# Sixty-four tokens of the second expert layer on fetched rows, the other 192 with merged high and low parts

## The reference

```python
q = (t @ w_q).reshape(b * n, PEER_HEADS, 2, PEER_KEY_DIM)        # 8 heads, keys of 128
s = jnp.einsum('thcd,hcnd->thcn', q, sub_keys)
sv, si = lax.top_k(s, PEER_TOPK)                                 # 16 of 128, twice
cand = (sv[:, :, 0, :, None] + sv[:, :, 1, None, :]).reshape(b * n, PEER_HEADS, PEER_TOPK * PEER_TOPK)
score, pos = lax.top_k(cand, PEER_TOPK)
expert = i1 * PEER_KEYS + i2                                     # of 16384 experts
gate = jax.nn.softmax(score)
act = gelu(einsum('td,thkd->thk', tb, take(u_tab, eb, axis=0)))
out = einsum('thk,thkd->td', gb * act, take(v_tab, eb, axis=0))
```

## Time and profile before

| | us |
|---|---|
| median of 3 runs | 3408.69 (3408.18 to 3410.98) |
| the profiled execution, its own time | 3414.44 |
| its span, first to last instruction | 3412.5 |
| PE busy | 3245.4 |
| DVE busy | 2377.2 |
| ACT busy | 1434.5 |
| POOL busy | 1061.1 |

### The profile page before, as it was taken

One profiled execution on the slowest core, in us unless ns is written; L12 is line 12 of the kernel. 1 busy time (PEld: TensorE's weight loads), 2 busy tenths in 40 slices (PEclk: granted clock), 3 DMA queues, 4 the chain that ended last, 5 costly groups with the idle time before them and its releaser, 6 DMA issues.

```text
span 3412.5 us, 53827 instructions
## 1 busy us (share of the span) xinstructions
PE 3245.4 (95%) x20582; PEld 2965.5 (87%) x20582; DVE 2377.2 (70%) x3931; ACT 1434.5 (42%) x1708; POOL 1061.1 (31%) x670
## 2 busy tenths in 40 slices
PE   7999889998999999999989999999988999999998
PEld 5999689755877999999989999997778999988787
DVE  6877477786753689988649989986664965016665
ACT  5435344323533333466523333324344468444443
POOL 0110000010000477777654335540001976740000
PEclk9999899999999999999999999999999999999999
DMA  8874157451022377799999999983114669768875
GB/s 318 334 295 167 50 203 247 160 191 50 1 75 93 116 270 244 260 374 382 361 349 390 381 391 409 409 337 111 38 61 156 230 210 307 257 233 288 305 287 205
DMA packets 305190, 814.27 MB, mean 239 GB/s; under 512 B 21760, under 2 KB 188928, under 8 KB 253696
## 3 DMA queue, kind: packets, MB, share of 16 engines
q1 hardware_dynamic: 241856, 583.07, 47.4%
q0 software_dynamic: 58752, 213.94, 16.6%
q10 hardware_dynamic: 4416, 15.05, 1.1%
HBM read 722.84 MB, written 89.13 MB: 238 GB/s over the span
## 4 chain that ended last, share of the span: by engine, by line
PE 76%; DVE 14%; DMA 5%; ACT 2%; issue 2%; POOL 0%; SPq 0%; DVEq 0%; ACTq 0%; POOLq 0%
PE ps L2747 18%; PE ps L3060 11%; PE ps L3052 9%; PE ps L861 7%; PE ps L1687 5%; PE ps L872 4%; DMA arena<-activations 3%; PE ps L2309 3%; PE ps L318 3%; PE ps L1429 2%; PE ps L2769 2%; PE ps L1411 2%; DVE arena L2785 2%; PE ps L2149 1%; PE ps L977 1%
## 5 line engine op out<-in xcount | busy, mean ns | idle before, releaser
L2747 PE MATMUL ps<-xT_split,arena_split 128*128 128x384 f32 (+1 forms) x4096 | 917.1, 312 | 17.1 <-POOL arena_split L2720 10.4
L2720 POOL TENSOR_TENSOR arena_split<-ring,arena_split 128x1024 fp32r<-128x1024 f32 x256 | 631.7, 2477 | 932.7 <-ACT arena_split L2674 931.6
L2747 PEld LDWEIGHTS ps<-xT_split,arena_split 128*128 128x128 f32 x4096 | 698.1, 191 | 18.6 <-issue 15.8
L2747 PE MATMUL ps<-hT_split,arena_split 128*128 128x384 f32 (+1 forms) x2048 | 635.4, 310 | 0.0
L3060 PE MATMUL ps<-arena_split 128*128 128x384 f32 x3072 | 535.4, 335 | 11.6 <-DVE arena_split L3012 11.6
L3060 PEld LDWEIGHTS ps<-arena_split 128*128 128x128 f32 x3072 | 534.8, 188 | 12.2 <-issue 11.7
L285 DVE TENSOR_TENSOR arena_split<-ring,arena_split 128x2048 fp32r<-128x2048 f32 x128 | 292.9, 2291 | 247.4 <-ACT arena_split L279 246.6
L2985 ACT ACTIVATE arena_split<-ring 128x2048 fp32r<-128x2048 f32 x128 | 245.5, 1918 | 492.3 <-PE ps L3060 283.3
L279 ACT ACTIVATE arena_split<-ring 128x2048 fp32r<-128x2048 f32 x128 | 244.5, 1915 | 379.1 <-PE ps L861 133.3
L2747 PEld LDWEIGHTS ps<-hT_split,arena_split 128*128 128x128 f32 x2048 | 392.3, 192 | 0.0
L3009 DVE TENSOR_TENSOR arena_split<-ring,arena_split 128x2048 fp32r<-128x2048 f32 x128 | 293.1, 2290 | 99.5 <-ACT arena_split L2985 98.5
(11 more groups left out here) (318 smaller groups left out, 5098.5 us busy)
## 6 DMA issues: line engine op xcount, KB each, us to landing
ring<-in_weights SPq DMA_DIRECT2D x396, 1024.0 KB
arena<-in_side_weights POOLq DMA_DIRECT2D x152, 512.0 KB, 5.6
gates<-arena SPq DMA_DIRECT2D x48, 512.0 KB
arena<-gates SPq DMA_DIRECT2D x32, 768.0 KB
arena<-activations SPq DMA_DIRECT2D x64, 384.0 KB
activations<-arena SPq DMA_DIRECT2D x128, 128.0 KB
gates<-arena SPq DMA_DIRECT2D x16, 1024.0 KB
arena<-gates SPq DMA_DIRECT2D x64, 256.0 KB
```

Source lines behind the costliest of these rows:

```text
L2720: pool.tensor_tensor(low, self.raw(f)[:, j, :], high.bitcast(F32), ALU.subtract)\
L2747: mm = pe.matmul(k.ps[:, j, 0:self.T], self.u[:, 2 * (f % 2) + j, a, t * P:(t + 1) * P], self.h[b][:, t, :], start=n == 0, stop=n == 3 * D ...
```

## The change

Layer two now takes the fetched way for its first 64 tokens and the dense way for the other 192 (`SPREAD = 64`, `T = 192`). Each of the 64 tokens is spread over two partitions, 64 picked rows on each, so that there are 64 fetches of u and 64 of v, each 128 rows of 4 KB (512 KB). `dots_of` takes the dot products in the lot stretch, at lot `n` all rows `s` with `24 * s // 64 <= n` (two or three a lot). Seven row buffers in the hidden stage, five in the values stage.

For the 192 dense tokens the high and low parts of the activations lie side by side, and one product with the high weights streams both (384 columns); a second product takes the low weights with the high activations (192 columns). So a half is 16 products, not 24. The high-times-low part lands in PSUM beside the rest and must be added: ACT copies it out (L2808) and PE adds it back with a product with the identity (`fix`, in the middle of the next half) before the gelu. In the values stage v is now the weight in the same two products, and a 64-column product with a 0/1 `selector` adds the fetched rows' sum; `PeerAddSpread` adds each of eight tiles to x as soon as PE has it.

The gates are built in 24 lots, one a pair in pairs 28 to 51 (`ROUTE_PAIRS` 24 becomes 28), and 12 pairs follow without lots. In these stretches DVE takes low parts off POOL: those of every second pair in the lot stretch, and all after it (`on_dve`). The copy of x to DRAM and back is dropped in layer two. In layer one nothing moves but that the lot stretch is written out, not looped.

```diff
-ROUTE_PAIRS = (32, 24)
+ROUTE_PAIRS = (32, 28)
+LOTS_PER_PAIR = (2, 1)
...
+class SpreadHidden:
+    N_BUFFERS = 7
...
+        self.lot_of = [lots * s // self.n for s in range(self.n)]
...
+    def gpsimd(self, pool, pair):
+        hidden, rows = self.hidden, self.k.io["u_rows"]
+        first = hidden.route_pairs // 2
+        if pair < first:
+            return
...
+        while self.issued < self.n:
+            s, b = self.issued, self.issued % self.N_BUFFERS
+            before = s - self.N_BUFFERS
+            ready = first + s if before < 0 else hidden.route_pairs + self.lot_of[before] // hidden.per_pair + 2
+            if ready > pair and pair < hidden.pairs - 1:
+                return
+            if before >= 0:
+                pool.wait_ge(self.dotted.sem, self.dotted.at(before + 1))
+            pool.indirect_dma_start(self.buffers[b], None, rows, bass.IndirectOffsetOnAxis(self.index[:, s:s + 1], 0),
+                                    element_offset=P * P * D).then_inc(self.landed[b].sem, 16)
+            self.issued += 1
...
+    def dots_of(self, dve, lot):
+        while self.taken < self.n and self.lot_of[self.taken] <= lot:
+            s = self.taken
...
+            dve.wait_ge(landed.sem, landed.at(16 * (s // self.N_BUFFERS + 1)))
+            dve.scalar_tensor_tensor(row, row, 1.0, self.own, ALU.mult, ALU.mult, accum_out=self.dots[:, s:s + 1])\
+               .then_inc(self.dotted.sem, 1)
...
+    def on_dve(self, c):
+        if not self.merged:
+            return False
+        return c >= self.lots_to or c >= self.route_pairs and (c - self.route_pairs) % 2 == 1
...
             for j in range(2):
                 pool.wait_ge(self.u_high.sem, c * 2 + self.u_high.at(j + 1))
+                if c and self.on_dve(c - 1):
+                    pool.wait_ge(k.chunk_products, c + self.g)
...
+        for c in range(self.pairs):
+            if not self.on_dve(c):
                 body(c, c, 0, 4)
+            self.gather.gpsimd(pool, c)
...
+        def merged_products(c, f, j):
...
+            for t in range(DT):
+                pe.matmul(both, self.u[:, u, 0, t * P:(t + 1) * P], self.h_both[:, t], start=t == 0, stop=True,
+                          skip_group_check=True)
+                mm = pe.matmul(both[:, 1, :], self.u[:, u, 1, t * P:(t + 1) * P], self.h_both[:, t, 1, :], start=False,
+                               stop=True, skip_group_check=True)
+                if t == 3 and (j or not first(c, 1)):
+                    fix(c * 2 + (j - 1), 1 - j)
...
+            if self.merged:
+                gather.dots_of(dve, n)
+                c = self.route_pairs + n
+                if self.on_dve(c):
+                    u_lows(c)
...
+        def u_lows(c):
+            for j in range(2):
+                dve.wait_ge(self.u_high.sem, self.u_high.at(2 * c + j + 1))
+                dve.wait_ge(k.chunk_products, c + self.g)
```

More of the change, by code:

```diff
@@ L2607, in walk @@
     def walk(self, eng, body, between=None, lots=None, after=None):
-        def both(*pair):
-            for j in range(2):
-                body(*pair, halves=(j,))
-                lots(*pair, halves=(j,))
         if body:
@@ L2743, in body @@
                     pe.wait_ge(self.gelus.sem, c * 2 + self.gelus.at(j - 1))
+                if self.merged:
+                    merged_products(c, f, j).then_inc(self.u_products.sem, 1)
+                    if isinstance(c, int) and c == self.pairs - 1 and j:
+                        fix(c * 2 + 1, 1)
+                    continue
                 n = 0
@@ L3022, in vector @@
             self.gather.add(dve, PAIRS)
+            self.finish(dve, (self.back, 16), (self.products, self.pairs))
         else:
-            walk(dve, 0, self.pairs, 4, body)
-        self.finish(dve, (self.back, 16), (self.products, self.pairs))
+            self.gather.select(dve)
+            n = self.gather.rows_total
+            for c in range(self.pairs):
+                body(c, c, 0, 4)
+                self.gather.add(dve, n * c // (self.pairs - 4) if c < self.pairs - 4 else n)
+            self.finish(dve)
     def gpsimd(self, pool):
```

412 lines of the change are left out of this document (276 added, 136 removed).

## The result

The change makes the kernel slower: 3493.03 us median of four runs (3483.68 to 3511.63) beside 3409.84 (3408.18 to 3415.75), ratio 1.0242, 95% interval 1.0207 to 1.0276. The profiled execution took 3489.81 us, its span 3488.0, where the prediction's sum for the profiled execution was 3425.4. So 64 us are to be found.

The account below looks back on a forecast made before the run. PE was taken to end last in all three stretches, POOL close behind while routing. Hidden +37, gap +3, values -28, end -1 give +11 us on 3408.7: 3419 us, slower by 0.3%, range 3375 to 3455.

Parts of the forecast that it names:

- The sign: Whole kernel: slower, by 0.3%; slower by more than 0.2% had a chance of 0.47.
- the ring: Lot stretch: DVE low part, POOL low parts, row fetch, dots and lots wait in a circle, 18.5 to 20 us each turn.
- L: Lot stretch: time from POOL issuing an even lot's last row until DVE takes it, set at 5.0 us.
- The price of 192 columns: PE, hidden and values stages: a product 192 columns wide takes 0.112 us, between 0.093 and 0.120.
- the time from the last ring to the end of the hidden products: Hidden stage: from 3012, pair 51 done at 3019, then twelve pairs without lots in 57 us, ending at 3077.
- the gap ahead of the values stage: Between hidden and values stages: 8.3 us before, plus 1.2 for the last fix and 1.7 for fetches beside gate loads.
- the end: After the values stage: turn and copies go, adds per tile outrun PE's last pair; 9.5 us instead of 10.5.
- Step one: Values stage: transfers of 2.0 MB set the pace at 4.95 us a pair, above PE, two buffers and DVE; 325.5 us.
- Step two: Lot stretch: an odd lot's two or three rows have landed when DVE needs them, so its dots take 2.5 or 3.75 us.
- The rival with late rows: Lot stretch: rows land as late as with loaded queues; L = 8 makes 3452 us, 12.9 makes 3506; chance 0.15.
- Step three: End of routing: DVE's routing has a few small instructions more, done by 2752; POOL sets the pace, first lot at 2783.
- T: Lot stretch: moment DVE has made the first low part of an odd pair; 2797 at pair 29, 3012 at pair 51.

Follow-up runs that it names:

- 4: Changed kernel with each u row from the eighth on issued one pair earlier in the hidden stage: 3440.24 us, ratio 1.0069.
- 5: Changed kernel with POOL making all low parts in the lot stretch and DVE none: 3439.97 us, ratio 1.0086.
- 1: Changed kernel with layer two's values-stage activations loaded ahead of the next 1 MB chunk, not behind it: 3455.04 us, ratio 1.012.
- 2: Changed kernel without 59 of the 64 fetches of v rows, DVE adding the first five again and again: 3458.14 us, ratio 1.0123.
- 3: Changed kernel with values-stage activations loaded ahead of the chunk and 59 of 64 v row fetches left out: 3456.91 us, ratio 1.0127.
- 7: Changed kernel with POOL waiting, ahead of each routing low part, for its own last one, leaving a gap: 3490.65 us, ratio 1.0231.
- 10: Changed kernel with activations loaded first, u rows a pair earlier, POOL waiting for DVE at two places and gaps in eight pairs: 3389.8 us, ratio 0.9926.

## Why the prediction was wrong

**What was right.** The sign, to which the prediction gave no more than 0.47, and the mechanism with the highest weight: the ring stands in the trace with all its links, L is 5.0 in the mean, as taken, PE is busy 64% in it (about 60% forecast), and two cuts at different links (4, 5) both open it. The price of 192 columns (0.1116), merged and low product together 0.286 us from start to start, the time from the last ring to the end of the hidden products (68 us for 65), the gap ahead of the values stage (9 for 11), the end (7.3 for 9.5).

**Step one that failed: the values stage, "Transfers ... That is the largest"**, 35 us. The list of what could set a pair's pace had PE, two buffers, DVE and bytes; it left out how long a transfer takes from issue to landing when its issue itself waits for the work two pairs back. Shown by 1: the order of two loads alone moves the stage from 360 to 321. The trace of before held the circle too, hidden. SP's last small load of a turn, the use that waits for it, and DVE's next low part:

```profile
3203.63 0.33 SPq L2957 DMA_DIRECT2D arena<-gates  x1
...
3208.72 0.69 DVE L3007 TENSOR_TENSOR arena<-arena 128x512 f32<-128x512 f32 x1 [0.41 <-DMA arena<-gates]
...
3210.86 2.29 DVE L3009 TENSOR_TENSOR arena_split<-ring,arena_split 128x2048 fp32r<-128x2048 f32 x1 [1.44 <-ACT arena_split L2985]
```

A turn took 10.88 us there (3202.18 to 3213.06, twice PE's 5.44 a pair), of which DVE stood 1.44 for ACT: the circle alone was some 9.4, 4.7 a pair. It came up for two reasons: PE's share fell to 4.6, and with the fetches of rows in the queues the time from issue to landing grew from 5.1 us (3203.63 to 3208.72) to 6.6 to 8.7. Take either away, the order (1) or the rows' bytes (2), and the stage falls to 321. The 4.95 us a pair is near the 5.0 of experiment 1 only by chance: without the rows' bytes and with the loads first the two buffers still give 4.83 (3), so most of it is not bytes.

**Step two: "whose rows were issued 1.2, 2.4 and 3.6 us later and have landed meanwhile"**, 20 us. They had not. The rows that an odd lot waited for, second to fourth of a burst, were used 7.4 to 10.7 us after their issue, where the ring as drawn leaves the fourth some 7.6 (by its own terms), and DVE stood 1.7 us a ring for them; POOL waits 0.45 more for ACT's second high part. So a ring takes 21.3, not 19.5. The rival with late rows had the direction but the wrong place: the first row of a burst landed as forecast, the ones issued behind it late.

**Step three: the start of the lots**, 11 us at pair 29 (T at 2808.4, not 2797). "DVE's routing has a few small instructions more" counted DVE's work and not what POOL does to it. Before, POOL stood 0.15 to 0.57 us for ACT ahead of 23 of its 50 low parts up to 2769. The instruction that is held took 2.36 and 2.26 us in its two executions of layer two, both times until the low part in progress ended and such a gap came (the expectation of 7 gives 0.29 and 2.36; the 0.29 is not of layer two):

```profile
2664.62 2.40 POOL L2720 TENSOR_TENSOR arena_split<-ring,arena_split 128x1024 fp32r<-128x1024 f32 x1 [0.47 <-ACT arena_split L2674]
2664.82 2.36 DVE L2809 TENSOR_TENSOR arena<-arena 128x128 f32<-128x128 f32 x1
2667.51 2.46 POOL L2720 TENSOR_TENSOR arena_split<-ring,arena_split 128x1024 fp32r<-128x1024 f32 x1 [0.48 <-ACT arena_split L2674]
```

The change made PE faster than POOL, so these gaps closed. That gaps prevent the long hold is shown: 7 and 10 change only when POOL's low parts start, and in the profiles of the six kernels with such gaps all 12 executions in layer two took 0.3 to 2.3 us, while 9 of the 16 in the eight kernels without them took 29 to 34. Why the other 7 of those got their turn within 1.2 us, also beside a stream without gaps, stays open. The rest of the late start, some 6 us (lots begin 162.2 us after POOL's first low part in 10, 156.1 in the forecast), is still there with few gaps; ACT's exponentials stand behind high parts of pair 28 in its order and DVE needs 6 us from them to the first lot, but no run took this apart.

The ring cost (21.3 - 15.6) x 11 = 63 us in the trace and 53 in the time (in the profile of 4 two instructions were held, and its lots began 9.5 us later), the circle of loads 38, the held instruction some 7 to 10. Without the three the changed kernel takes 3389.8 us, 0.7% less than the kernel before.

## What to carry to other kernels

When a change takes work off the bounding engine, look for every circle that its length had covered: for each transfer write down what its issue waits for, add the time to landing behind whatever else the queues then carry, and divide by the buffers. A burst of fetches has one such time for its first and a longer one for its fourth. Put the small load that is needed first ahead of the large one that is needed later. And an engine that now runs without gaps may stop its neighbour, so a new bound on POOL is a question to DVE's instructions with two inputs in SBUF.

## What the runs showed of the hardware

- A DVE instruction of 0.29 us with two inputs in SBUF was held for 34.0 us while POOL ran two-input instructions without a gap, about fourteen of them; so in the profiles of all eight kernels without gaps, once in seven of them (33.9 to 34.0), twice in one (29.5 and 34.0). In those seven the other of the two executions in layer two took 1.2 us, though POOL had no gap there either. If POOL waits for its own last instruction ahead of each, that leaves gap enough: then this instruction was held for one POOL instruction at most (2.3 us). By the Trainium skill (SBUF — State Buffer, "Who interferes with whom") a DVE instruction with two SBUF inputs and a GpSimd instruction that reads SBUF exclude each other for the whole instruction. The trace agrees that one is held, but the long hold lasted through some fourteen instructions of the other, not one.
- A load of 192 KB behind 1 MB in one queue, with fetches of rows beside them, landed 6.6 to 8.7 us after its issue; ahead of the 1 MB it took 5.4 in the median, and behind it without the fetches 4.9. A DMA share of 0.95 at 354 GB/s stood beside the first, and yet 400 GB/s went through after the change of order. The share alone is no proof of a bound by bytes.
- A DVE instruction does not show that it is held as idle time: the 34 us count as busy.
- Of fetches of 512 KB issued 1.25 us apart, the first was used 4.5 to 5.6 us after its issue, and those waited for behind it 7.4 to 10.7 us after theirs.
